# Scan stage of a hybrid SSD and mLSTM decoder layer: decay masks on GpSimd, one activation table set, sample states updated one chunk later

## What is computed

```
acs  = cumsum(dt * a);  lmat = exp(where(t >= s, acs[t] - acs[s], -inf))
y    = ((C B^T) * lmat * dt) x + (C h) * exp(acs)
h    = h * exp(acs[T-1]) + B^T (exp(acs[T-1] - acs) * dt * x)            # SSD
dmat = where(t >= s, bcs[t] - bcs[s] + i[s], -inf);  att = (q k^T) * exp(dmat - m_t)
num  = att v + w_inter * (q c);  den = att.sum + w_inter * (q n);  out = num / max(|den|, exp(-m_t))
c    = w_old * c + k^T (w_s * v)                                         # mLSTM
```

## Time and profile before

| | |
|---|---|
| median of 3 runs | 3622.85 us (3621.53 to 3631.1) |
| the profiled execution | 3604.28 us, span 3602.2 us, granted TensorE clock 0.952 |
| busy, share of the span | PE 89%, DVE 71%, POOL 47%, ACT 27% |
| scan stage | 648 to 1023 us; one chunk every 39.8 us |

### The profile page before, as it was taken

One profiled execution on the slowest core, in us unless ns is written; L12 is line 12 of the kernel. 1 busy time (PEld: TensorE's weight loads), 2 busy tenths in 40 slices (PEclk: granted clock), 3 DMA queues, 4 the chain that ended last, 5 costly groups with the idle time before them and its releaser, 6 DMA issues. The chain is left out here.

```text
span 3602.2 us, 45960 instructions
## 1 busy us (share of the span) xinstructions
PE 3198.9 (89%) x15207; PEld 2173.5 (60%) x15207; DVE 2552.8 (71%) x5367; ACT 968.8 (27%) x2152; POOL 1706.9 (47%) x1424
## 2 busy tenths in 40 slices
PE   6998999688888888888887765999999999999998
PEld 6998999677643223322324443777776766777765
DVE  6662000488848788888889997777877777877777
ACT  2111111366511111111127877111111111111111
POOL 2333221122203566676675555555555555555553
PEclk9999999799989999999998878999999999999999
DMA  3334332677765899999998989999999999999996
GB/s 95 91 89 139 115 112 98 207 254 250 265 227 191 307 355 352 340 356 337 347 350 321 321 334 366 393 385 391 388 407 391 395 379 374 393 400 391 395 383 244
DMA packets 392154, 1074.27 MB, mean 298 GB/s; under 512 B 55000, under 2 KB 157400, under 8 KB 384912
## 3 DMA queue, kind: packets, MB, share of 16 engines
q0 software_dynamic: 186624, 679.56, 50.4%
q1 hardware_dynamic: 131160, 298.78, 23.0%
q10 hardware_dynamic: 74168, 93.48, 7.3%
HBM read 978.48 MB, written 93.05 MB: 297 GB/s over the span
## 5 line engine op out<-in xcount | busy, mean ns | idle before, releaser
L1425 POOL DMA_INDIRECT ub<-in_peer_u,gix x640 | 691.4, 1080 | 634.6 <-DVE hid L1695 424.1
L2040 PE MATMUL PB<-vbd,wd 128*128 128x512 f32 x1536 | 681.3, 593 | 0.0
L2027 PE MATMUL PB<-xds,uts 128*128 128x384 f32 x3072 | 568.7, 339 | 0.0
L2027 PEld LDWEIGHTS PB<-xds,uts 128*128 128x128 f32 x3072 | 531.0, 189 | 0.5 <-issue 0.5
L1425 POOL DMA_INDIRECT vbf<-in_peer_v,gixv x300 | 350.6, 1169 | 277.5 <-PE PB L2067 134.6
L1425 POOL DMA_INDIRECT vbf<-in_peer_v,gix x340 | 396.8, 1167 | 163.0 <-issue 99.8
L2040 PEld LDWEIGHTS PB<-vbd,wd 128*128 128x128 f32 x1536 | 282.7, 191 | 307.0 <-issue 307.0
L2067 PE MATMUL PB<-vbf,dg 128*64 128x512 f32 x1200 | 331.3, 676 | 138.0 <-DMA vbf<-in_peer_v,gixv 113.7
L1656 DVE TENSOR_TENSOR uts<-PB,uts 128x512 fp32r<-128x512 f32 x256 | 175.7, 687 | 294.3 <-ACT uts L1873 274.8
L1695 DVE CUSTOM_DVE_ANT_0 ub<-ub,x1g 128x1024 f32<-128x1024 f32 x257 | 313.2, 1221 | 77.1 <-DMA ub<-in_peer_u,gix 67.8
L1873 ACT CAST uts<-PB 128x512 fp32r<-128x512 f32 x256 | 150.1, 586 | 640.2 <-PE PB L2016 617.9
(11 more groups left out here) (390 smaller groups left out, 5341.8 us busy)
## 6 DMA issues: line engine op xcount, KB each, us to landing
vbd<-in_peer_v SPq DMA_DIRECT2D x128, 512.0 KB
x1d<-in_peer_u SPq DMA_DIRECT2D x96, 512.0 KB
gd_d<-stag ACTq DMA_DIRECT2D x12, 2048.0 KB
gbd<-gd_d SPq DMA_DIRECT2D x16, 1536.0 KB
ubd<-in_peer_u SPq DMA_DIRECT2D x32, 512.0 KB
wtr<-in_w_tok SPq DMA_DIRECT2D x12, 1024.0 KB, 8.1
tok_d<-stg ACTq DMA_DIRECT2D x96, 128.0 KB, 1.7
rb<-rows_d SPq DMA_DIRECT2D x8, 1536.0 KB, 8.7
```

The lines of the kernel that those rows point to most:

```text
L1425: pool.indirect_dma_start(out=buf, out_offset=None, in_=a[table], in_offset=bass.IndirectOffsetOnAxis(ap=index, axis=0)).then_inc(done, 16)
L2027: last = T.matmul(PB[:, 6, 0:TD], uts[:, b % 2, ul, k, :], xds[:, xl, k, :], start=(k, n) == (0, 0), stop=(k, n) == (KD - 1, 2))
L2040: last = T.matmul(PB[:, 2 * d + n, :], wd[:, b % 2, d * CH:(d + 1) * CH], vbd[b % 8][:, n * 512:(n + 1) * 512], start=b == 0, stop=b == NB ...
```

## The change

The change moves six things in the scan stage.

1. `masked_rows` goes from VectorE (in `head_out`) to GpSimd, at the head of its chunk, behind waits for rb and for the ni product of the chunk before. GpSimd's dx now also waits for xdt.
2. ScalarE loads, once, a table set that has Ln and Exp.
3. ScalarE's copies and small exponentials of a chunk stand ahead of the roots of the chunk before; kT is copied before the third exponential of L instead of the fifth.
4. The place of the masks in `head_out` is taken by st += t3. The rest of sample i's work (cs += t4, t3 = st * C and its row sum, now `sample_end`) is done in chunk i + 1, between L998 and L1005; for the last sample at once.
5. TensorE's product of sample i moves from the end of chunk i to chunk i + 1, between ys and hn, into bank 2; the last one stands after the loop.
6. ScalarE's copy of that product goes to a tile of its own and stands, with its five DMAs, between the decays of st and cs of chunk i + 1. SyncE's loads of a sample also wait for `red` of the sample two before.

```diff
--- before.py
+++ after.py
@@ -522,6 +522,7 @@
+    nrow = sb("nrow", [P, DK])
@@ -529,11 +530,11 @@
-        "act_xt act_small act_l act_qk act_l2 act_mt act_nx dve_l pool_arg pool_xdec pool_dx pool_hs pool_og "
+        "act_xt act_small act_l act_qk act_l2 act_mt act_nx pool_l pool_arg pool_xdec pool_dx pool_hs pool_og "
...
-        "ld zo bct bcc bcd qk qkc exp arg nst cur decay outer st_new red c_new num numc num_out num_in den end").split()}
+        "ld zo bct bcc bcd qk qkc exp arg nst cur decay outer st_new red c_new summed num numc num_out num_in den end").split()}
@@ -545,15 +546,14 @@
-    def masked_rows(dve, i):
-        dve.wait_ge(s["rb"], 16 * (i + 1))
-        if i == 0:
-            dve.wait_ge(s["mask"], 2)
-        free(dve, s["pe_ni"], i)
-        V.tensor_tensor(L[:, :, :], rb[:, 0:NH + MH, :],
-                        maskp[:, :].unsqueeze(1).to_broadcast([P, NH + MH, CH]), ALU.add).then_inc(s["dve_l"], 1)
...
-    def head_out(dve, ch, r, em, n, y, num, qn, den, og):
+    def masked_rows(pool, i):
...
+        pool.wait_ge(s["rb"], 16 * (i + 1))
+        free(pool, s["pe_ni"], i)
+        G.tensor_tensor(L[:, :, :], rb[:, 0:NH + MH, :],
+                        maskp[:, :].unsqueeze(1).to_broadcast([P, NH + MH, CH]), ALU.add).then_inc(s["pool_l"], 1)
...
+    def head_out(dve, ch, r, em, n, y, num, qn, den, og, meanwhile=None):
@@ -566,8 +566,8 @@
-        if n + 1 < NCH:
-            masked_rows(dve, n + 1)
+        if meanwhile:
+            meanwhile()
@@ -618,7 +618,7 @@
-                free(sp, s["dve_l"], i)
+                free(sp, s["pool_l"], i)
@@ -635,6 +635,7 @@
+                free(sp, ss["red"], i - 1)
@@ -648,7 +649,7 @@
-            sp.wait_ge(s["dve_l"], NCH)
+            sp.wait_ge(s["pool_l"], NCH)
@@ -690,6 +691,16 @@
+            def sample_num(n):
...
+                pe.wait_ge(ss["c_new"], n + 1)
+                for e in range(2):
+                    for k in range(KT):
+                        for h in range(MH):
+                            last = T.matmul(PB[32 * h:32 * h + B, 2, e * P:(e + 1) * P], qs[:, h * KT + k, :],
+                                            cs[n % 2][:, h * KT + k, e * P:(e + 1) * P], start=k == 0, stop=k == KT - 1, tile_position=(0, 32 * h))
+                last.then_inc(ss["num"], 1)
@@ -701,7 +712,6 @@
-                free(pe, ss["numc"], i)
@@ -741,12 +751,15 @@
+                pe.wait_ge(s["dve_att"], i + 1)
+                if i:
+                    sample_num(i - 1)
...
-                pe.wait_ge(s["dve_att"], i + 1)
+                free(pe, ss["numc"], i)
@@ -766,17 +779,10 @@
-                pe.wait_ge(ss["c_new"], i + 1)
-                pe.wait_ge(s["dve_c1"], i + 1)
-                for e in range(2):
-                    for k in range(KT):
-                        for h in range(MH):
-                            last = T.matmul(PB[32 * h:32 * h + B, e, 0:P], qs[:, h * KT + k, :],
-                                            cs[q][:, h * KT + k, e * P:(e + 1) * P], start=k == 0, stop=k == KT - 1, tile_position=(0, 32 * h))
-                last.then_inc(ss["num"], 1)
...
-            pe.wait_ge(ss["numc"], NCH)
+            pe.wait_ge(s["dve_c1"], NCH)
+            sample_num(NCH - 1)
...
+            pe.wait_ge(ss["summed"], NCH)
@@ -792,6 +798,7 @@
+            pe.wait_ge(ss["numc"], NCH)
@@ -805,7 +812,7 @@
+            S.preload_act_table_set("natural_log_exp_and_others")
@@ -832,10 +839,21 @@
+            def sample_out(n):
+                act.wait_ge(ss["num"], n + 1)
+                free(act, ss["num_out"], 64 * n)
+                S.copy(nrow[:, :], PB[:, 2, 0:DK]).then_inc(ss["numc"], 1)
+                act.wait_ge(ss["numc"], n + 1)
+                for h in range(MH):
+                    act.dma_start(num_d[n:n + 1, h * DK:(h + 1) * DK], nrow[32 * h + n:32 * h + n + 1, :]).then_inc(ss["num_out"], 16)
+                act.dma_start(o["s_c"][bass.ds(n, 1)].rearrange("b (j p) v -> p (b j) v", p=P), cs[n % 2][:, :, :]).then_inc(s_out[n % 2], 16)
...
+            def ssd_store(n):
+                act.wait_ge(ss["st_new"], n + 1)
+                act.dma_start(o["s_ssd"][bass.ds(n, 1)].rearrange("b (j p) n -> p (b j) n", p=P), st[n % 2][:, :, :]).then_inc(s_out[n % 2], 16)
...
-                if i:
-                    root(act, P, i - 1)
@@ -853,9 +871,11 @@
-                act.wait_ge(s["dve_l"], i + 1)
+                if i:
+                    root(act, P, i - 1)
+                act.wait_ge(s["pool_l"], i + 1)
...
-                    if h == 4:
+                    if h == 2:
@@ -871,6 +891,7 @@
+                    ssd_store(i - 1)
@@ -878,8 +899,9 @@
+                if i:
+                    sample_out(i - 1)
...
-                free(act, ss["num_out"], 64 * i)
@@ -891,16 +913,10 @@
-                act.wait_ge(ss["st_new"], i + 1)
-                act.dma_start(o["s_ssd"][bass.ds(i, 1)].rearrange("b (j p) n -> p (b j) n", p=P), st[q][:, :, :]).then_inc(s_out[q], 16)
-                act.wait_ge(ss["num"], i + 1)
-                S.copy(t4[:, 0, :].rearrange("p (e n) -> p e n", e=2), PB[:, 0:2, 0:P]).then_inc(ss["numc"], 1)
-                act.wait_ge(ss["numc"], i + 1)
-                for h in range(MH):
-                    act.dma_start(num_d[i:i + 1, h * DK:(h + 1) * DK], t4[32 * h + i:32 * h + i + 1, 0, :]).then_inc(ss["num_out"], 16)
-                act.dma_start(o["s_c"][bass.ds(i, 1)].rearrange("b (j p) v -> p (b j) v", p=P), cs[q][:, :, :]).then_inc(s_out[q], 16)
...
+            ssd_store(NCH - 1)
+            sample_out(NCH - 1)
@@ -933,16 +949,16 @@
-                pool.wait_ge(s["rb"], 16 * (i + 1))
+                masked_rows(pool, i)
...
+                pool.wait_ge(s["dve_xdt"], i + 1)
...
-                pool.wait_ge(s["dve_xdt"], i + 1)
@@ -977,8 +993,17 @@
+            def sample_end(n):
...
+                dve.wait_ge(ss["outer"], n + 1)
+                V.tensor_tensor(cs[n % 2][:, :, :], cs[n % 2][:, :, :], t4[:, :, :], ALU.add).then_inc(ss["c_new"], 1)
+                dve.wait_ge(ss["st_new"], n + 1)
+                bc_n = bb[n % 2][:, :].rearrange("p (c g n) -> p c g n", c=2, g=NG)
+                V.tensor_tensor(groups(t3[:, :, :]), groups(st[n % 2][:, :, :]), bc_n[:, 1].unsqueeze(2).to_broadcast([P, NG, 4, NST]), ALU.mult).then_inc(ss["red"], 1)
+                dve.wait_ge(ss["red"], n + 1)
+                V.tensor_reduce(ych[:, :, bass.ds(n, 1)].rearrange("p a b -> p (a b)"), t3[:, :, :], AX, ALU.add).then_inc(ss["summed"], 1)
...
-            masked_rows(dve, 0)
@@ -999,6 +1024,9 @@
+                if i:
+                    sample_end(i - 1)
+                    dve.wait_ge(ss["summed"], i)
@@ -1018,13 +1046,6 @@
-                dve.wait_ge(ss["decay"], i + 1)
-                V.tensor_tensor(st[q][:, :, :], st[q][:, :, :], t3[:, :, :], ALU.add).then_inc(ss["st_new"], 1)
-                dve.wait_ge(ss["st_new"], i + 1)
-                V.tensor_tensor(groups(t3[:, :, :]), groups(st[q][:, :, :]), bcq[:, 1].unsqueeze(2).to_broadcast(over), ALU.mult).then_inc(ss["red"], 1)
-                dve.wait_ge(ss["outer"], i + 1)
-                V.tensor_tensor(cs[q][:, :, :], cs[q][:, :, :], t4[:, :, :], ALU.add).then_inc(ss["c_new"], 1)
@@ -1034,11 +1055,15 @@
-                    if half == 0:
-                        dve.wait_ge(ss["red"], i + 1)
-                        V.tensor_reduce(ych[:, :, bass.ds(i, 1)].rearrange("p a b -> p (a b)"), t3[:, :, :], AX, ALU.add)
...
+                def new_state():
+                    dve.wait_ge(ss["decay"], i + 1)
+                    V.tensor_tensor(st[q][:, :, :], st[q][:, :, :], t3[:, :, :], ALU.add).then_inc(ss["st_new"], 1)
+                    if i == NCH - 1:
+                        sample_end(i)
...
-                head_out(dve, ch, P, e_em[q][:, :], i, ysb[:, :], num[:, :, :], num[:, :, DK], den[:, :], og[:, :])
+                head_out(dve, ch, P, e_em[q][:, :], i, ysb[:, :], num[:, :, :], num[:, :, DK], den[:, :], og[:, :], new_state)
```

## The result

| | before | after |
|---|---|---|
| median | 3622.36 us (4 runs, 3621.53 to 3631.1) | 3576.22 us (4 runs, 3565.09 to 3586.75) |
| the profiled execution | 3604.28 us | 3586.75 us |
| second comparison of the two programs | 3614.83 (25 runs) | 3592.72 (8 runs) |
| third comparison | 3615.53 (11 runs) | 3587.49 (6 runs) |

The ratio is 0.9874, 95% interval 0.985 to 0.9897: faster by 46 us, where I had forecast 3600 and a range of 3586 to 3619. The two further comparisons gave 0.9937 (0.9916 to 0.9959) and 0.9926 (0.9905 to 0.9947): 22 and 28 us. The profiled execution of before is not one of its four runs and lies 18 us under their median, that of after is one of its four and lies 11 over, so the two spans differ by 17 us only.

The account below looks back on a forecast made before the run. No engine was full; a ring of waits set the scan chunk's 39.8 us. First chunk -4, seven chunks -28 and last chunk +9 gave -23: 3581 on the profiled execution, 3600 as median, range 3586 to 3619.

Parts of the forecast that it names:

- the walk: One new scan chunk reckoned step by step over all engines: 34.4 us at full clock, where the old chunk took 39.8.
- T: The end of L568 (dve_var) of the chunk before, from which the steps of a chunk are timed.
- wait ahead of c1: Late in the chunk, TensorE's c1 waits for ScalarE's nx, late behind the sample's product: a new stop of 2.0 us.
- next T: End of the chunk: c1 and c2 at 2.0 each, num hidden, then 4.2 more, giving 34.4 us a chunk.
- clock term: TensorE's low clock after stops, costing c2 1.4 and q·k 1.0 a chunk: bounds 34.4 to 36.8, taken 35.8.
- First chunk: First scan chunk: num no longer stands behind the three sample sums (4.6 us), c2 follows: 4 us earlier.
- Last chunk: After the last L568: all the sample's work falls there, 9 us later, bounds 7 to 12.
- Masks: The mask add on GpSimd, some 4.75 us long behind ni, done before it is needed: price 0.
- DMAs: A sample's loads and SyncE's new wait for red: in time for ScalarE, price 0, bounds 0 to 3 us.
- loads late: Sample loads or sums come late under DMA pressure: period 38.3, -3.5 us, no change (3619); chance 0.17.
- Table loads stay: ScalarE keeps its table loads, about 1.8 us more before L: period 37.6, -10 us (3613); chance 0.04.
- The lock: GpSimd's masks lock VectorE out, up to 4.75 us lost: period 41, +13 us (3636), slower; chance 0.08.

Follow-up runs that it names:

- a_state: The kernel before with only the sample's work moved (masks, table set and order of roots as before): chunk 40.7 us against 39.9, one run 3632.0 us.
- t_two: The kernel after with the common table set and the order of the roots undone, so sample's move and masks only: chunk 38.2 us, one run 3615.13 us.
- u_tables: The kernel after without the one table set loaded in advance, so two table loads a chunk: chunk 36.6 us against 34.2, one run 3595.24 us.
- u_state: The kernel after with the sample's work all back in its own chunk: chunk 42.4 us against 34.2, one run 3646.62 us.

## Why the prediction was wrong, by its steps

The sign, the mechanism and the walk were right; the forecast of 3600 was missed by 24 us, the range by 10. Of the walk, measured in the chunk shown above (T = 815.91):

| step | predicted | measured |
|---|---|---|
| copies and small exponentials end | T - 0.1 | T - 0.05 |
| roots end | T + 0.4 | T + 0.5 |
| L ready | T + 7.7 | T + 7.7 |
| y starts | T + 10.1 | T + 10.1 |
| sample's product ends | T + 16.8 | T + 16.6 |
| ni ends | T + 24.1 | T + 24.0 |
| nx ready | T + 26.1 | T + 26.2 |
| wait ahead of c1 | 2.0 | 2.20 |
| next T | T + 34.4 | T + 34.2 |

(By its own terms the walk's last sum is 26.1 + 4.0 + 4.2 = 34.3. Five other chunks took 33.9 to 34.0.) In one row luck helped: y and ys ended at T + 15.6 instead of T + 15.3, and the sample's product took 1.06 instead of 1.5. And VectorE's gate ended at T + 24.4, not T + 23.7, since t3 = B x stood beside GpSimd's og and took 2.01 instead of 1.2; the wait for nx covered it.

**The step that failed is the clock term.** The walk gave 34.4 with no loss; I then kept 1.4 of 2.4, "nearer the upper since a stop stays", and forecast 35.8. Measured: 0 in six chunks. Seven times 1.6 is 11 us, and with it the sum is -34, as the stage showed. Its own bound was right (34.4), the choice in it wrong. In one chunk of seven the loss did come: the stop there was 1.92, c1 took 3.25, c2 2.38 and the period 35.60. Over the three profiles of the kernel after it came in four chunks of 21, each 35.6 to 35.7 long, a mean of 0.3 a chunk. That stop was no longer than the others, so one such stop in a chunk may or may not bring the low clock; in a_state and t_two, with three and two stops of over 1 us, q·k had it every time, but in u_tables, where 2.08 ahead of q·k is the only such stop in the first half of the chunk, it came in five chunks of seven too. What decides, length or place or number of the stops, these runs do not settle. I had argued from a single stop in the kernel before, 3.8 long.

**The clock term is not all of the miss.** With -34 the forecast would have been 3589, inside the range. The measured 3576 lies 12 us beyond what the stage shows, and this part is not in the scan stage: in the one profiled execution the rest of the kernel was even 12 us longer than before's. The two later comparisons, at 22 and 28 us, would have fallen into the range. Where the 12 us of the first one come from stays open.

**The range was too narrow.** Its best case was -35 with 2 us for the spread of the runs. Runs of one program spread by 20 to 43 us, the two profiles' remainder of the kernel by 12, and three comparisons of the same two programs gave 22, 28 and 46. The best case stood where the stage came out, and next to nothing was kept for the measurement.

**First chunk**: -4 predicted, -3.9 in both repeats (65.2 against 69.1; against the second profile of before -5.9), -0.9 in the first profile. **Last chunk**: +9 predicted, measured 10.0 to 10.7 in the three profiles, with the low clock that I had put into the bound of 12. **Masks**: price 0, right; length 4.75 estimated, 5.70 measured: 2560 columns took 2.2 ns each where 1024 take 1.9. **DMAs**: price 0, right, at a share of 0.81: no decay of st or t4 waited for a load. **Rivals**: loads late, not seen. Table loads stay, did not happen; u_tables gives some 2 for the loads where I had 1.8, and 2.4 with the low clock. The lock did not bind with the masks in after, where the mask add starts 1.0 behind the start of the last gate operation, so one that starts 1 us earlier would, by the turns seen in u_state, hold that operation; u_state shows it real and larger than priced (5.3 on one instruction, 43.4 a chunk where the masks meet the sums, in place of 41).

## What to carry to other kernels

Walk one period in absolute times from the rows, and treat the clock as a separate term with two values and keep both in the range: here a stop of 1.7 to 2.2 us in a chunk of 34 left it full in 17 chunks of 21, and one of 3.8 never did. An edit that removes one long wait can lose by lengthening several small ones. Parts of such a change are not additive: adding one alone and undoing it from the whole gave -0.8 and 8.2 for the same part, so run both, and read single chunks where a mean is odd. Where VectorE starts an operation on two SBUF tiles beside a running GpSimd operation, let it end only behind that one. And keep some room in the range for the spread of the runs.

## What the runs showed that I had not expected

14 fillers, 3.3 us of work that computes nothing, made the kernel before 2.2 us a chunk faster. The sample's move alone made the chunk 0.8 us longer, though it removed the longest wait in it. A GpSimd mask add of 2560 columns took 5.70, and 6.51 where VectorE's st += t3 was still running at its start (876.24 to 877.46). And work of a last chunk moved ahead of a wait costs nearly what it cost behind it (1.7 of 9.2 gained) where no other work can cover it.
